# Modulation rows of a two-layer diffusion block made in pairs of steps, one PSUM bank for two steps

## The reference, cut to what matters

```python
silu_c = jax.nn.silu(c)              # (1, 1024)
silu_cc = jax.nn.silu(c_ctx)         # (1024,)
for l in range(DEPTH):               # DEPTH = 2
    mod_x = (silu_c @ w_ada[l] + b_ada[l])[:, None, :]      # 6144 values
    mod_c = (silu_cc @ w_ada[l] + b_ada[l])[None, None, :]
    sh1_x, sc1_x, gt1_x, sh2_x, sc2_x, gt2_x = jnp.split(mod_x, 6, axis=-1)
    ...
    hx = modulate(rms_norm(x, g_norm1[l]), sh1_x, sc1_x)
    ...   # projection, three attention mixers, residual with gt1, norm, conv ffn, residual with gt2
```

## Time and profile before

| | us |
|---|---|
| three runs, median (lowest, highest) | 2297.65 (2296.98, 2303.8) |
| the profiled execution's own time | 2298.63 |
| its span, first to last instruction | 2296.8 |
| PE busy | 2151.5 (94%) |
| DVE busy | 1532.2 (67%) |
| ACT busy | 1152.5 (50%) |

### The profile page before, as it was taken

One profiled execution on the slowest core, in us unless ns is written; L12 is line 12 of the kernel. 1 busy time (PEld: TensorE's weight loads), 2 busy tenths in 40 slices (PEclk: granted clock), 3 DMA queues, 4 the chain that ended last, 5 costly groups with the idle time before them and its releaser, 6 DMA issues.

```text
span 2296.8 us, 42538 instructions
## 1 busy us (share of the span) xinstructions
PE 2151.5 (94%) x17528; PEld 1987.3 (87%) x17528; DVE 1532.2 (67%) x2285; ACT 1152.5 (50%) x1917; POOL 565.1 (25%) x668
## 2 busy tenths in 40 slices
PE   6999989999999998989998989999998998999997
PEld 4985668999999995679997979999997888998997
DVE  3657766777777765757777678855555777965554
ACT  3533444554655552555556546554444655564443
POOL 0021330333233102213321043213331124312331
PEclk8998999999999997999999999999999999999999
DMA  8535454555465453435563525554553443454552
GB/s 326 165 129 202 154 196 156 175 194 183 148 204 190 148 165 115 162 110 191 189 195 99 165 93 189 173 171 147 186 188 109 143 146 132 166 175 141 189 193 83
DMA packets 103200, 378.22 MB, mean 165 GB/s; under 512 B 11584, under 2 KB 11744, under 8 KB 101984
## 3 DMA queue, kind: packets, MB, share of 16 engines
q1 hardware_dynamic: 101520, 367.31, 47.2%
q10 hardware_dynamic: 1488, 8.20, 0.9%
HBM read 374.42 MB, written 1.05 MB: 163 GB/s over the span
## 4 chain that ended last, share of the span: by engine, by line
PE 36%; issue 8%; DVE 5%; POOL 3%; ACT 3%; POOLq 0%; DVEq 0%; ACTq 0%
PE ps L395 11%; PE ps L397 10%; PE ps L396 10%; DVE WL L1577 2%; POOL R L2539 1%; PE ps L454 1%; POOL R L2497 1%; ACT WH L967 1%; DVE RST L1613 1%; PE ps L409 1%; DVE R L1587 1%; PE ps L410 1%; PE ps L417 1%; DVE TMP L1587 1%; POOL X L2300 0%
## 5 line engine op out<-in xcount | busy, mean ns | idle before, releaser
L395 PE MATMUL ps<-X,WH 128*128 128x256 f32 x4384 | 1241.8, 283 | 16.9 <-DVE WL L1577 16.0
L396 PE MATMUL ps<-X,WH 128*128 128x256 f32 x4384 | 1227.9, 280 | 0.0
L397 PE MATMUL ps<-X,WL 128*128 128x256 f32 x4384 | 1226.1, 280 | 0.0
L1577 DVE TENSOR_TENSOR WL<-RAW,WH 128x1024 fp32r<-128x1024 f32 (+2 forms) x608 | 782.5, 1307 | 455.3 <-ACT WH L967 454.6
L395 PEld LDWEIGHTS ps<-X,WH 128*128 128x128 f32 x4384 | 826.2, 188 | 31.5 <-DVE WL L1577 21.2
L396 PEld LDWEIGHTS ps<-X,WH 128*128 128x128 f32 x4384 | 826.6, 189 | 1.4
L397 PEld LDWEIGHTS ps<-X,WL 128*128 128x128 f32 x4384 | 826.4, 188 | 0.0
L967 ACT ACTIVATE WH<-RAW 128x1024 fp32r<-128x1024 f32 (+2 forms) x608 | 624.1, 1046 | 270.5 <-PE ps L397 263.5
L1105 ACT ACTIVATE PB<-ps,SM 128x512 f32<-128x512 f32 (+1 forms) x152 | 87.8, 584 | 165.4 <-DVE SM L1747 165.1
L2342 POOL TENSOR_SCALAR R<-CONS,SM 128x128 f32<-128x128 f32 x128 | 84.4, 670 | 351.0 <-DVE SM L1757 351.0
L2436 POOL TENSOR_TENSOR TMP<-TMP 128x256 f32<-128x256 f32 x66 | 49.0, 743 | 445.2 <-ACT TMP L1289 445.2
(11 more groups left out here) (188 smaller groups left out, 2257.1 us busy)
## 6 DMA issues: line engine op xcount, KB each, us to landing
RAW<-w_dram SPq DMA_DIRECT2D x674, 512.0 KB, 3.9
RAW<-w_dram SPq DMA_DIRECT2D x16, 480.0 KB, 3.2
BIG<-big_dram ACTq DMA_DIRECT2D x4, 1024.0 KB, 5.1
RAW<-w_dram SPq DMA_DIRECT2D x8, 320.0 KB, 2.7
RAW<-w_dram SPq DMA_DIRECT2D x6, 384.0 KB, 3.1
XT<-x_dram ACTq DMA_DIRECT2D x2, 1024.0 KB, 10.7
CONS<-con_dram ACTq DMA_DIRECT2D x1, 1105.0 KB, 4.9
out_dram<-XT SPq DMA_DIRECT2D x1, 1024.0 KB, 3.9
```

The costliest lines, as they stand in the source:

```text
L395: e.matmul(out, a.hi, b.hi, start=start and i == 0, stop=False, skip_group_check=open_bank)
L396: e.matmul(out, a.hi, b.lo, start=False, stop=False, skip_group_check=open_bank)
L397: last = e.matmul(out, a.lo, b.hi, start=False, stop=stop and i == n - 1, skip_group_check=open_bank)
L1577: e.tensor_tensor(weights(i).lo, raw(i), weights(i).hi.bitcast(F32), ALU.subtract).then_inc(*w_lo.mark(i))
```

## The change

Two steps, one after the other in `k.todo`, become a pair that shares one bank. The 256 columns of a step are cut into halves of 128: parts x = 0, 1 of the array take the two column halves for two of the four k chunks, parts 2, 3 for the other two, and the two k chunks of one part are summed in PSUM (`n`). The stationary operand is a window of 32 columns into a strip of 34 (`CVEC[step]`), so that step 0 puts its two streams into rows 0, 1 of each part and step 1 into rows 2, 3; step 1 adds to the same bank. Then one copy of 128 columns, one matmul with eight columns of `pick`, and one bias addition serve both steps. On PE the waiting turn is now called ahead of the first step of a pair, where it was called behind each step; DVE calls it ahead of its `used()` calls, where it stood behind them. Steps outside the attention and the start use bank 7 as well.

```diff
-        SCZ = R[:, 7168:7424].rearrange("p (k m) -> p k m", k=8)
+        SCZ = R[:, 7168:7440].rearrange("p (k m) -> p k m", k=8)
+        CVEC = [SCZ[:, :, 2 - 2 * step:34 - 2 * step] for step in range(2)]
...
   # PE, ada_turn
-                for h in range(2):
-                    last = e.matmul(bank.ap[:, 256 + 2 * h:258 + 2 * h], b.ap[:, 128 * h:128 * h + 128], con("pick"), start=True, stop=True)
-                last.then_inc(*adaturn.mark(l, c))
+                e.matmul(bank.ap[:, 256:264], b.ap[:, 0:128], con("pick"), start=True, stop=True).then_inc(*adaturn.mark(l, c))
...
   # PE, ada_step
-            def ada_step(ring=PS, ahead=3):
+            def ada_step(ring=k.ada, ahead=3):
                 l, c = k.todo.pop(0)
-                bank = ring.take()
+                step = int(k.first is not None)
+                if not step:
+                    ada_turn()
+                    k.first = (l, c), ring.take()
+                place, bank = k.first
                 for h in range(2):
                     i = feed.next(ahead)
...
-                    for c4 in range(4):
-                        last = e.matmul(bank.ap[32 * c4:32 * c4 + 32, 0:256], SCZ[:, 4 * h + c4], w[:, c4], start=h == 0, stop=h == 1)
+                    for n in range(2):
+                        for x in range(4):
+                            c4 = 2 * (x // 2) + n
+                            last = e.matmul(bank.ap[32 * x:32 * x + 32, 0:128], CVEC[step][:, 4 * h + c4], w[:, c4, 128 * (x % 2):128 * (x % 2) + 128],
+                                            start=not step and h == 0 and n == 0, stop=step == 1 and h == 1 and n == 1)
                     last.then_inc(*lin.mark(i))
                     feed.release(i)
-                ada_turn()
-                k.pend = ((l, c), k.rows.take(), bank)
+                if step:
+                    k.pend, k.first = (place, k.rows.take(), bank), None
...
   # DVE, ada_turn (one addition, 128x8, when the two steps are neighbours) and ada_step
+                step = int(k.first is not None)
+                if not step:
+                    ada_turn()
+                    k.first = (l, c), ring.take()
                 used(ahead)
                 i = used(ahead)
-                ada_turn()
-                b = k.rows.take()
-                q.wait_ge(*lin(i))
-                wait(b.free)
-                e.tensor_copy(b.ap, bank.ap[:, 0:256]).then_inc(*modded.mark("row", l, c))
+                if step:
+                    (place, bank), k.first = k.first, None
+                    b = k.rows.take()
+                    q.wait_ge(*lin(i))
+                    wait(b.free)
+                    e.tensor_copy(b.ap[:, 0:128], bank.ap[:, 0:128]).then_inc(*modded.mark("row", *place))
```

More of the change, by code:

```diff
@@ L317, in __init__ @@
                 self.todo = [(l, c) for l in range(DEPTH) for c in range(24)]
-                self.pend = None
+                self.pend, self.first = None, None
                 self.mods = {}
@@ L478, in ada_step @@
                     q.wait_ge(*raw_in(i))
-                    if h == 0:
+                    if h == 0 and not step:
                         q.wait_ge(*gated("c"))
                         wait(bank.free)
-                    for c4 in range(4):
-                        last = e.matmul(bank.ap[32 * c4:32 * c4 + 32, 0:256], SCZ[:, 4 * h + c4], w[:, c4], start=h == 0, stop=h == 1)
+                    for n in range(2):
[3 more added lines that the diff above has]
+                                            start=not step and h == 0 and n == 0, stop=step == 1 and h == 1 and n == 1)
                     last.then_inc(*lin.mark(i))
                     feed.release(i)
-                ada_turn()
-                k.pend = ((l, c), k.rows.take(), bank)
+                if step:
+                    k.pend, k.first = (place, k.rows.take(), bank), None
             def parts_of(tag):
@@ L1023, in rstd, with ada_step @@
                     e.activation(out.ap, self.bank.ap[:, 0:256], ACT.Sqrt, scale=1.0 / size, bias=eps).then_inc(*roots.mark(self.tag))
-            def ada_step(ring=PS, ahead=3):
+            def ada_step(ring=k.ada, ahead=3):
                 k.todo.pop(0)
-                ring.take()
+                if k.first is None:
+                    ring.take()
+                    k.first = True
+                else:
+                    k.first = None
                 used(ahead)
@@ L1167, in scalar @@
             q.wait_ge(*small("zero"))
-            e.activation(SCZ[:, :, 0:2], par("c").rearrange("p (k s) -> p k s", s=2), ACT.Silu).then_inc(*gated.mark("c"))
+            e.activation(SCZ[:, :, 2:4], par("c").rearrange("p (k s) -> p k s", s=2), ACT.Silu).then_inc(*gated.mark("c"))
             for c in range(8):
@@ L1617, in ada_turn @@
                     return
-                l, c, bank = k.pend
+                (l, c), c2, bank = k.pend
                 k.pend = None
@@ L1621, in ada_turn, with ada_step @@
                 q.wait_ge(*((s_par2, 16) if l else (s_par, 16)))
-                parts = bank.ap[:, 256:260].rearrange("p (h s) -> p s h", h=2)
-                b_ada = par("b_ada", l)[:, 2 * c:2 * c + 2].unsqueeze(1).to_broadcast([128, 2, 2])
-                e.tensor_tensor(MODS[l][:, :, 2 * c:2 * c + 2], parts, b_ada, ALU.add).then_inc(*modded.mark(l, c))
+                parts = bank.ap[:, 256:264].rearrange("p (j s) -> p s j", s=2)
+                for j, n, x in ((c, 4, 0),) if c2 == c + 1 else ((c, 2, 0), (c2, 2, 2)):
+                    b_ada = par("b_ada", l)[:, 2 * j:2 * j + n].unsqueeze(1).to_broadcast([128, 2, n])
+                    last = e.tensor_tensor(MODS[l][:, :, 2 * j:2 * j + n], parts[:, :, x:x + n], b_ada, ALU.add)
+                last.then_inc(*modded.mark(l, c))
                 k.mods[l] = modded(l, c)
-            def ada_step(ring=PS, ahead=3):
+            def ada_step(ring=k.ada, ahead=3):
                 l, c = k.todo.pop(0)
-                bank = ring.take()
+                step = int(k.first is not None)
+                if not step:
+                    ada_turn()
+                    k.first = (l, c), ring.take()
                 used(ahead)
                 i = used(ahead)
-                ada_turn()
-                b = k.rows.take()
-                q.wait_ge(*lin(i))
-                wait(b.free)
-                e.tensor_copy(b.ap, bank.ap[:, 0:256]).then_inc(*modded.mark("row", l, c))
-                b.free = [adaturn(l, c)]
-                k.pend = (l, c, bank)
+                if step:
[4 more added lines that the diff above has]
+                    e.tensor_copy(b.ap[:, 0:128], bank.ap[:, 0:128]).then_inc(*modded.mark("row", *place))
+                    b.free = [adaturn(*place)]
+                    k.pend = place, c, bank
             def modulate(tag, st, g, shift, scale, to, ready, lag=1):
@@ L2752, in constants @@
     put("eps", EPS)
-    put("pick", np.tile(np.eye(32)[:, 0:2], (4, 1)))
+    pick = np.zeros((2, 2, 32, 2, 2, 2))
+    for step, half, st in np.ndindex(2, 2, 2):
+        pick[:, half, 2 * step + st, step, half, st] = 1.0
+    put("pick", pick.reshape(128, 8))
     sel, selT = np.zeros((128, 4, 2, 32)), np.zeros((128, 4, 128))
```

8 lines of the change are left out of this document (4 added, 4 removed).

## The result

The changed kernel takes 2276.1 us (median of 4 runs, 2268.8 to 2278.1) where the kernel before took 2297.3 beside it: ratio 0.990, 95% interval 0.987 to 0.993. That is faster by 21 us; the forecast was 2281. So the direction and most of the size were right, and the gain was some 4 to 6 us larger than the sum said. The ratios are worked out from the single runs and are not simply the quotients of the two medians. The profiled execution took 2276.16 us with a span of 2274.3 against 2296.8, 22.5 less.

The account below looks back on a forecast made before the run. PE was taken to bound one-map units, DVE two-map units, PE-DVE handovers the loops, transfers and then DVE's order the start; -7.0 - 7.0 - 5.8 + 2.4 = -17.4 us from 2298.63 gave 2281, range 2275 to 2291.

Parts of the forecast that it names:

- Products: A step's matmuls on PE: 32 records of 128 columns for 16 of 256, costing 0.04 us more a step.
- the rival in which records can't start closer than 0.055 us: Products issue-bound: each step grows by 0.86 us, total 2309 us, slower than before; chance 0.06.
- One-map units: Attention units where PE never rests: 11 pairs save 0.67 us each, less 0.4 taken back; -7.0 us.
- Two-map units: Attention units where DVE sets the pace: shorter waits and copies save 1.5, 2.6 and 2.9 us; -7.0 us.
- a term it had counted only in the second stream: Second stream's two-map units: step 1 no longer waits for the bias of step 0, 1.2 us saved.
- the clock as a rival: PE's lower-clock stretches: one or two more give 2285 to 2288, one fewer 2278; chance 0.17 that it costs this.
- Loops: Normalising loops where PE and DVE hand over: left-out turns save 3.6 in layer 0, 1.6 + 0.6 in layer 1; -5.8 us.
- The start: Turn ahead of step 6 delays slots and pieces; last bias addition 46.0 against 43.56, +2.4 us, bounds 0 and +4.5.
- the three signs by which the prediction was to be wrong: A step over 1.4 us, attentions gaining less than 10 us together, or the start losing more than 5.
- 50.4 us in which PE stood idle ahead of a turn: Profile figure before the change: PE idle ahead of a turn until the copy was done, 48 times.
- the forecast that it would fall under 20 from 50: Expected sign in the profile: PE's idle time ahead of turns down from 50 to under 20 us.
- a thing that takes 0.4 us back: Turn behind the last step of the second and third attention waits for DVE's splits anyway; 0.4 us off the one-map gain.

Follow-up runs that it names:

- e4: Kernel before, each product of a step cut into two of 128 columns (32 records for 16), nothing else changed; 2299.0 us, ratio 1.001.
- e3: Changed kernel plus four unread records of the turn's shape on PE wherever a turn was taken out, waiting for nothing new; 2279.1 us, ratio 0.994.
- e12: Changed kernel with the edits of e2 and e3 together, the four records also waiting for the copy of constants; 2290.9 us, ratio 0.997.
- e2: Changed kernel, VectorE also waiting for each pair's first step, then copying 256 constant columns to unused columns; 2271.5 us, ratio 0.989.
- e8: Changed kernel without column halves: products and copy of 256 columns, a turn of two matmuls, two additions a pair; 2275.5 us, ratio 0.990.
- e7: Kernel before, with only a step's turn moved ahead of its products on TensorE; 2301.1 us, ratio 1.001.
- e6: Changed kernel, VectorE's copy of a pair's rows moved ahead of that step's two splits, TensorE's order kept; 2262.1 us, ratio 0.984.
- e1: Changed kernel, PE calling the waiting turn behind the products of a pair's first step, not ahead of them; 2266.8 us, ratio 0.988.
- e9: Kernel before, VectorE's copy and with it the bias addition moved ahead of the step's two splits; 2287.8 us, ratio 0.996.

## Why the prediction was right or wrong

**Products.** Right, and even less than the 0.04 us a step that was taken; the rival in which records can't start closer than 0.055 us is refuted twice, by the changed kernel and by e4. The 81 ns of the Trainium skill for a pair of load and matmul with 128 columns (TensorE: Matmul & The Clock Gate, Back-to-back issue gap) is not what four column parts show: 1.08 us less one record of 0.273, divided by 31, is 0.026 us a record.

**One-map units.** Right in mechanism and size: 0.73 us a pair against 0.67, 4.34 and 4.65 against 4.4 and 4.7; -6.2 in all against -7.0, since in each attention one pair waited for the bank (0.50, 0.31 and 0.62 us), which the sum had not. e3 confirms the larger term, a left-out turn of 0.53. e12 shows that there is also a second way to lose it, through VectorE.

**Two-map units, -7.0 forecast, -11.7 measured.** This is the step that failed: a right mechanism, mis-sized. By attention it was 1.5, 2.9 and 2.6 in the sum, and 3.7, 3.7 and 4.3 in the trace. The sum took the waits of VectorE for TensorE one by one, from a timeline in which one of the units was already at the full clock, and let each give its own length. It left out (a) that TensorE in turn waited for the bank, 1.9, 1.8 and 3.0 us in the three attentions, which fell to nothing, 0.6 and 0.9, a term it had counted only in the second stream, and (b) the clock: PE was busy all 12 us of the window at 1.2 GHz before, and the clock rose from 0.50 to 0.97. The prediction had the clock as a rival in both directions, and gave it only 2278 on this side. e3 gives 4.1 us of the 11.7 to the turns left out and what hangs on them; e2, e8 and e7 show nothing that can be told from the scatter for the wait and copy on VectorE, the halves and TensorE's order, and e12 nothing more for the two waits together. The other 7 us are, by elimination, the bank's wait at every second step, the clock, or both. No run restored that wait alone, so this is argued and not shown. That the waits' own lengths are not the size is seen in e6: its first two-map units wait 0.9 us for the bank and take 20.1 us, where the changed kernel has no such wait and takes 20.7, at the same clock of 0.92.

**Loops, -5.8 forecast, -7.8 measured.** 5.2 of it in layer 0, where 3.6 were forecast, and 2.6 in layer 1 for 2.2. The clock was taken as given; in layer 0's loop it was 0.86 before and is 1.00 in the changed kernel, and also in e3 and e12, which have the turns' records back. e3 puts 2.0 us back, e12 4.3, and TensorE's order by itself costs 3.8 (e7).

**The start, +2.4 forecast, +4.7 measured**, just outside the 4.5 that was given as its bound; counted from step 5, which came 0.7 us later, it is 4.1. The chain was the one described, and e1 removes it whole. Its sizes were off at three places: the turn came at 37.81 in place of 36.8, behind a copy at 37.47; the two steps behind it took 3.64 us, as PE had rested 5.5 us and ran at 1.2 GHz, where the slots were to be free 1.2 to 2.2 us behind the turn; and the pieces came at 42.55 and 45.08 in place of 41.4 and 42.7.

**The total is in part luck.** The two-map units, the loops and the rest gave 4.7, 2.0 and 1.5 us more than the sum had, the start and the one-map units 2.3 and 0.8 less; so errors of 8.2 and 3.1 us left one of 5. None of the three signs by which the prediction was to be wrong came: a step takes 1.08 us, the attentions gain 17.9, the start loses 4.7.

**The number used for the idle time was misread.** "50.4 us in which PE stood idle ahead of a turn" is the idle time of both of TensorE's rows in the profile, matmuls (PE) and weight loads (PEld), ahead of that line. The waits of the matmuls alone, over the whole span, are these, before and then after:

```profile
PE ps L468 <- DVE R L1636: 13.2, 9, 4.1
```

```profile
PEld ps L468 <- DVE R L1653: 30.1, 21, 6.1
PE ps L468 <- DVE R L1653: 18.6, 9, 5.7
```

The weight load waits while earlier matmuls still stream, and that time was never lost. The real one was 13.2 us, and rose to 18.6, 11.2 of it at the start. So the forecast that it would fall under 20 from 50 was empty: by line it is 48.8, as shown above. The sum did not use it, which is why the error did not reach the time.

**What was missed.** The prediction saw that the copy stands behind the splits at the start and behind the last steps of two attentions, and counted it as a thing that takes 0.4 us back. It was the largest cheap gain in reach: 9 us without the change (there with the bias addition), 14 with it.

## What to carry to other kernels

When work is taken from two engines that hand over to each other, list the waits in both directions, the one for the buffer too, before summing; and look at the granted clock of each unit that is summed and of what runs ahead of it, since here the lower clock began in the loop before the units. A wait in a queue is priced by what stands behind it: here a turn that had to wait anyway cost 5 us only because the steps that free the transfers' slots stood behind it. And a short copy for which another engine waits belongs ahead of long work that waits for transfers: two lines exchanged gave, on top of the change, as much as two thirds of it, and the best kernel of this study is the change with that exchange, 2260.7 to 2262.1 us.

## What the runs showed of the hardware

- Four column parts of 32 weight columns take short records almost for free: 32 float32 records of 128 moving columns in 1.08 us, 16 of 256 in 1.07 (e4 and the changed kernel, at a clock of 1.00).
- A long rest of TensorE was paid twice here. Windows of the changed kernel behind the rests of 5.50 and 3.31 us:

```profile
38.00:42.00 4.00, 3.98 (x66) 3.28 (x66) 1.30 (x2) 0.00 (x0) 0.00 (x0) 0.50 0.39 135
```

```profile
311.00:315.00 4.00, 4.00 (x24) 2.67 (x24) 1.23 (x5) 1.33 (x5) 1.19 (x2) 0.50 0.68 237
```

  and of e6 behind its 1.03 us:

```profile
305.00:309.00 4.00, 2.75 (x32) 2.01 (x31) 4.00 (x10) 1.69 (x7) 1.18 (x2) 1.00 1.01 344
```

  Records behind the long rests take 1.7 to 1.9 times their time (64 of them 3.64 us for 1.96, eight 1.12 for 0.66), behind the short one they do not. A long rest is not needed for it: the loop of layer 0 fell to the lower clock before with no wait over 0.65 us.
- In the first 12 us of two-map units PE was granted 0.50 in all four kernels with a turn for each step (before, e4, e7, e9), with records in flight all the time, and 0.72 to 0.97 in all ten with pairs. Within the ten the clock does not go with the turns' records: it is 0.73 and 0.74 with them (e3, e12) and 0.72 without (e8). What in the pairs brought it back is not shown.
- The same program differs from run to run by up to 21 us (before: 2285.6 to 2307.0 in 17 runs), about as much as the change is worth, so differences of under 5 us were read from the starts of rows within a stage and not from the medians.
